# Two fp32 products of a state-space layer become three fp32r passes, and the step is reordered

## The reference

```python
cb = jnp.einsum('bclgn,bcsgn->bclsg', cc, bc)
y_diag = jnp.einsum('bclsgr,bcsgrp->bclgrp', cb[..., None] * decay, xdt)
states = jnp.einsum('bclgn,bclgr,bclgrp->bcgrpn', bc, decay_to_end, xdt)   # "state" product
...
def step(carry, inp):
    st, dec = inp
    return carry * dec[..., None, None] + st, carry
...
y_off = jnp.einsum('bclgn,bcgrpn,bclgr->bclgrp', cc, prev, jnp.exp(a_cs))  # "offset" product
y = (y_diag + y_off) + d_skip * xs; y = y * silu(z); y = rms_norm(y)
```

## Time and profile before

| | |
|---|---|
| median of 3 runs | 2752.06 us (2752.05 to 2752.53) |
| profiled execution, its own time | 2754.46 us |
| its span | 2752.7 us |
| TensorE busy | 2710.4 us, 98% of the span |
| VectorE, ScalarE, GpSimd busy | 58%, 45%, 40% |
| mean granted TensorE clock | 0.997 of full |

### The profile page before, as it was taken

The page is one execution under the profiler, slowest core; times in us unless marked ns, Lnnn a source line. Parts: engine busy times, 40 slices in busy tenths (PEclk is TensorE's granted clock), DMA queues, the critical chain, the costliest instruction groups (busy, mean ns, idle before and its releaser), DMA issues.

```text
span 2752.7 us, 37252 instructions
## 1 busy us (share of the span) xinstructions
PE 2710.4 (98%) x13950; PEld 2234.5 (81%) x13950; DVE 1609.6 (58%) x2221; ACT 1234.6 (45%) x2414; POOL 1093.3 (40%) x798
## 2 busy tenths in 40 slices
PE   8999999999999999999999999999999999999998
PEld 6778778888788887888888888878888888888887
DVE  3589833567425665147763466664445666666666
ACT  2367734556424555145552644555445322222323
POOL 1356641132101322003324587865655435353434
PEclk9999999999999999999999999999999999999999
DMA  9687576645556445565436546674444942333323
GB/s 291 206 272 235 198 273 246 240 161 197 182 200 260 157 148 204 198 233 208 167 144 244 189 157 224 238 265 166 154 141 167 350 153 92 138 122 131 122 92 153
DMA packets 225490, 531.12 MB, mean 193 GB/s; under 512 B 14090, under 2 KB 98062, under 8 KB 215838
## 3 DMA queue, kind: packets, MB, share of 16 engines
q1 hardware_dynamic: 225310, 528.74, 53.6%
HBM read 382.74 MB, written 145.95 MB: 192 GB/s over the span
## 4 chain that ended last, share of the span: by engine, by line
PE 92%; ACT 2%; DVE 2%; DMA 1%; issue 1%; POOL 1%; SPq 0%; DVEq 0%; ACTq 0%; POOLq 0%
PE bank L2007 22%; PE bank L1975 21%; PE bank L1697 19%; PE bank L1741 13%; PE bank L1721 6%; PE bank L1819 2%; PE bank L1812 2%; PE bank L1638 1%; PE bank L1793 1%; PE bank L1800 1%; PE bank L1776 1%; ACT E L1388 1%; DMA w_scr<-w_both 1%; PE bank L1760 1%; PE bank L1930 0%
## 5 line engine op out<-in xcount | busy, mean ns | idle before, releaser
L1697 PE MATMUL bank<-hnT_hi,w_ring 128*128 128x512 f32 x1152 | 374.4, 396 | 1.4 <-DMA w_ring<-w_scr 1.3
L2126 DVE SCALAR_TENSOR_TENSOR acc<-pre,par,acc 128x512 f32<-128x512 f32 x240 | 216.3, 901 | 108.7 <-ACT pre L1250 103.0
L2007 PE MATMUL bank<-w_first,T_hi 128*128 128x512 f32 x896 | 276.0, 389 | 0.3 <-issue 0.3
L1697 PEld LDWEIGHTS bank<-hnT_hi,w_ring 128*128 128x128 f32 x1152 | 216.5, 188 | 46.5 <-ACT pre L1250 1.4
L1975 PE MATMUL bank<-T_hi,w_both 128*128 128x512 f32 x768 | 242.6, 390 | 0.6 <-DMA T_lo<-hn_scr 0.4
L1741 PE MATMUL bank<-w_ring,T_hi 128*128 128x512 f32 x768 | 242.0, 396 | 0.0
L2449 DVE TENSOR_TENSOR acc_th<-bank,acc_th 128x512 f32<-128x512 f32 x224 | 149.9, 686 | 153.5 <-PE bank L2007 153.3
L1003 POOL TENSOR_TENSOR small<-small 128x1 f32<-128x1 f32 (+1 forms) x71 | 17.4, 245 | 546.2 <-ACT yo L1333 340.0
L1697 PE MATMUL bank<-hnT_lo,w_ring 128*128 128x512 f32 x576 | 224.8, 390 | 0.0
L1721 PE MATMUL bank<-w_ring,hnT_hi 128*128 128x384 f32 x768 | 198.4, 339 | 0.0
L2007 PEld LDWEIGHTS bank<-w_first,T_hi 128*128 128x128 f32 x896 | 168.1, 188 | 35.6 <-issue 0.7
(11 more groups left out here) (289 smaller groups left out, 6242.5 us busy)
## 6 DMA issues: line engine op xcount, KB each, us to landing
w_ring<-w_scr SPq DMA_DIRECT2D x312, 512.0 KB, 4.2
T_scr<-stage SPq DMA_DIRECT2D x32, 1792.0 KB, 6.8
w_scr<-w_both SPq DMA_DIRECT2D x104, 512.0 KB, 4.3
pair_raw<-in_w_ff SPq DMA_DIRECT2D x36, 1024.0 KB, 5.5
third<-T_scr SPq DMA_DIRECT2D x28, 1024.0 KB, 4.9
pair_raw<-T_scr SPq DMA_DIRECT2D x28, 1024.0 KB, 4.8
sums<-sums_scr SPq DMA_DIRECT2D x64, 384.0 KB, 4.9
raw<-in_w_in SPq DMA_DIRECT2D x36, 512.0 KB, 6.9
```

The lines of the kernel that those rows point to most:

```text
L1697: mm = nc.tensor.matmul(bank[s][:, :], w[:, k, :], t[:, k, :], start=(k == 0 and j == 0), stop=(k == KT - 1 and j == 2))
L2007: mm = nc.tensor.matmul(bank[4 * half + t][:, :], a[:, k, tok], w[:, k, :], start=(SECOND[q % 7] not in GOES_ON and k == 0 and j == 0), st ...
L2126: ins = nc.vector.scalar_tensor_tensor(acc[:, s, 0:TB], pre[:, s, k:k + TB], w, acc[:, s, 0:TB], ALU.mult, ALU.add)
```

## The change

The state and the offset product each become three fp32r matmuls: high by high, high by low, low by high. The high parts are copies by ScalarE into fp32r tiles (B from the transposed bank, C, S and xw); the low parts are subtractions, B and xw on VectorE, C and S on GpSimd. `y_offset` of q waits for `s_split_lo`, the low part of S of step q; the state product waits for `xw_split_lo`. On TensorE the transposes of y move to one step later and to before the diagonal product, and the state product moves behind `slot1`, so that the fp32 work of a step stands in one piece. GpSimd's decay of S moves up to right behind the split. `state_add` moves ahead of the taps. The copies of the pool history go from VectorE to ScalarE. The split tiles lie in the space of h, so h is loaded during the output projection, behind the weights of its fifth unit.

```diff
 ScalarE, step q
-                        state_ps.wait(act, b, q)
                         ty_ready.wait(act, b, q)
                         xw_ready.wait(act, b, q)
-                        nc.scalar.activation(xb[:, :], bank[4 + q % 2][:, :], ACT.Copy
+                        nc.scalar.activation(b_both[q % 2][:, 0, :], bank[4 + q % 2][:, GW:GW + P],
+                                             ACT.Copy)
+                        nc.scalar.activation(xb[:, :], bank[4 + q % 2][:, 0:GW], ACT.Copy
                                              ).then_inc(xb_ready.sem, 1)
...
                         if q:
                             y_squares(b, q - 1)
+                        yoff_ps.wait(act, b, q)
+                        nc.scalar.activation(c_both[:, 0, :], group_tile(g, 1)[:, c * P:(c + 1) * P],
+                                             ACT.Copy)
+                        state_ready.wait(act, b, q)
+                        nc.scalar.activation(s_both[:, 0, :], S[:, g, :], ACT.Copy
+                                             ).then_inc(s_split_hi.sem, 1)
                         tanh(b, n1)
                         if q:
                             y_norm(b, q - 1)
+                        xw_ready.wait(act, b, q + 1)
+                        nc.scalar.activation(xw_both[:, 0, :], xw[:, :], ACT.Copy
+                                             ).then_inc(xw_split_hi.sem, 1)
...
-                        if q:
-                            y_high(b, q - 1)
+                        if q > 1:
+                            y_high(b, q - 2)
 GpSimd, step q (the inverse root of q-1 stands ahead of it, unchanged)
-                        steps.link(nc.gpsimd.tensor_tensor(by_head(ty[:, :]), by_head(xb[:, 0:GW]),
+                        steps.link(nc.gpsimd.tensor_tensor(by_head(ty[:, :]), by_head(xb[:, :]),
                                                            per_head(dsk, 0, g), ALU.mult))
+                        s_split_hi.wait(pool, b, q + 1)
+                        nc.gpsimd.tensor_tensor(c_both[:, 1, :], group_tile(g, 1)[:, c * P:(c + 1) * P],
+                                                c_both[:, 0, :].bitcast(F32), ALU.subtract)
+                        nc.gpsimd.tensor_tensor(s_both[:, 1, :], S[:, g, :],
+                                                s_both[:, 0, :].bitcast(F32), ALU.subtract
+                                                ).then_inc(s_split_lo.sem, 1)
+                        gains_ready.wait(pool, b, 1)
+                        s_split_lo.wait(pool, b, q + 1)
+                        nc.gpsimd.tensor_tensor(by_head(S[:, g, :]), by_head(S[:, g, :]),
+                                                per_head(cd, c, g), ALU.mult
+                                                ).then_inc(scd_ready.sem, 1)
 TensorE
-                def y_offset(b, q, g, c):
-                    state_ready.wait(pe, b, q)
-                    nc.tensor.matmul(bank[7][:, 0:GW], group_tile(g, 1)[:, c * P:(c + 1) * P],
-                                     S[:, g, :], start=True, stop=True).then_inc(yoff_ps.sem, 1)
+                def y_offset(b, q):
+                    s_split_lo.wait(pe, b, q + 1)
+                    for j, (i, o) in enumerate(((0, 0), (0, 1), (1, 0))):
+                        mm = nc.tensor.matmul(bank[7][:, 0:GW], c_both[:, i, :], s_both[:, o, :],
+                                              start=(j == 0), stop=(j == 2))
+                    mm.then_inc(yoff_ps.sem, 1)
...
+                def state(b, q):
+
+                    xw_split_lo.wait(pe, b, q + 1)
                     yo_ready.wait(pe, b, q + 1)
-                    nc.tensor.matmul(bank[7][:, 0:GW], xb[:, GW:GW + P], xw[:, :],
-                                     start=True, stop=True).then_inc(state_ps.sem, 1)
+                    for j, (i, o) in enumerate(((0, 0), (0, 1), (1, 0))):
+                        mm = nc.tensor.matmul(bank[7][:, 0:GW], b_both[q % 2][:, i, :],
+                                              xw_both[:, o, :], start=(j == 0), stop=(j == 2))
+                    mm.then_inc(state_ps.sem, 1)
...
                         if n1 is not None:
                             unit(b, n1)
+                        if q > 1:
+                            y_transposes(b, q - 2)
                         if q:
-                            slot3(b, q - 1)
+                            diagonal(b, q - 1)
                         slot1(b, q, g, c)
+                        if q:
+                            state(b, q - 1)
                         for n in n2:
                             unit(b, n)
-                        y_offset(b, q, g, c)
-                        if q:
-                            y_transposes(b, q - 1)
-                    slot3(b, STEPS - 1)
+                        y_offset(b, q)
+                    y_transposes(b, STEPS - 2)
+                    diagonal(b, STEPS - 1)
+                    state(b, STEPS - 1)
 VectorE
                             y_finish(b, q - 1)
+                            state_add(b, q - 1)
                         taps(b, n1)
-                        if q:
-                            state_add(b, q - 1)
...
+                        nc.vector.tensor_tensor(b_both[q % 2][:, 1, :], bank[4 + q % 2][:, GW:GW + P],
+                                                b_both[q % 2][:, 0, :].bitcast(F32), ALU.subtract)
...
+                        if n1 is not None:
+                            xw_low(b, q)
                         yoff_ps.wait(dve, b, q + 1)
 SyncE, output projection
+                            if (d, i) == (0, 4):
+                                yoff_ps.wait(sp, b, STEPS)
+                                state_ps.wait(sp, b, STEPS)
+                                sp.dma_start(h[:, :, :], x_in[0, b * TB:(b + 1) * TB, :].rearrange(
+                                    "(t p) d -> p t d", p=P)).then_inc(h_loaded.sem, 16)
```

More of the change, by code:

```diff
@@ L97, in __init__, with mark, wait, link @@
         self.eng, self.sem, self.n = eng, sem, 0
-    def link(self, ins):
+    def mark(self, ins):
         self.n += 1
         ins.then_inc(self.sem, 1)
-        self.eng.wait_ge(self.sem, self.n)
+        return self.n
+    def wait(self, n):
+        self.eng.wait_ge(self.sem, n)
+    def link(self, ins):
+        self.wait(self.mark(ins))
 ITEMS_G = 5 + CH
@@ L201, in build @@
         E = nc.alloc_sbuf_tensor_at("E", [P, HEADS_PER_GROUP, P], F32, offset=T_lo_at)
-        xb = sb("xb", [P, GW + P])
+        xb = sb("xb", [P, GW])
         xdt = sb("xdt", [P, GW])
@@ L245, in build @@
         quad = at("quad", [P, 4, 4, TB], R0 + 32768)
+        s_both = at("s_both", [P, 2, GW], h_at, F32R)
+        xw_both = at("xw_both", [P, 2, GW], h_at + 3072, F32R)
+        c_both = at("c_both", [P, 2, P], h_at + 6144, F32R)
+        b_both = [at(f"b_both{i}", [P, 2, P], h_at + 7168 + 1024 * i, F32R) for i in range(2)]
         t1_at = at("t1_at", [P, 4, TB], R0 + 65536)
@@ L350, in build @@
         g_ready = sig("g_ready", STEPS)
+        s_split_hi = sig("s_split_hi", STEPS)
+        s_split_lo = sig("s_split_lo", STEPS)
+        xw_split_hi = sig("xw_split_hi", STEPS)
+        xw_split_lo = sig("xw_split_lo", STEPS)
         yoff_ps = sig("yoff_ps", STEPS)
@@ L390, in build @@
         f_sumsq, f_rstd, f_out, out_stored = sem("f_sumsq"), sem("f_rstd"), sem("f_out"), sem("out_stored")
-        dve_sem, pool_sem = sem("dve_step"), sem("pool_step")
+        dve_sem, pool_sem, act_sem = sem("dve_step"), sem("pool_step"), sem("act_step")
         rows_loaded, consts = sem("rows_loaded"), sem("consts")
@@ L1048, in _ @@
                                                 ).then_inc(ty_ready.sem, 1)
[L1050 to L1055, removed]
                     inverse_root(b, rsy[:, :], ssy[:, :], ssy_ready, STEPS, rsy_ready, 1)
@@ L1220, in _ @@
                 high_part(act, 1)
+                steps = Steps(act, act_sem)
                 def evac(b, v):
@@ L1243, in evac @@
                         w3 = par[:, W_CONV + 60 + ct:W_CONV + 61 + ct]
-                        nc.scalar.activation(pre[:, s, 0:3], hist[:, ct, :], ACT.Copy
-                                             ).then_inc(hist_read.sem, 1)
+                        hist_read = steps.mark(nc.scalar.activation(
+                            pre[:, s, 0:3], hist[:, ct, :], ACT.Copy))
                         nc.scalar.activation(acc[:, s, 0:TB], ps, ACT.Identity, scale=w3,
                                              bias=par[:, W_BIAS + ct:W_BIAS + ct + 1])
-                        hist_read.wait(act, b, sum(conv_tile(m) is not None for m in range(n + 1)))
+                        steps.wait(hist_read)
                         nc.scalar.activation(hist[:, ct, :], ps[:, TB - 3:TB], ACT.Copy)
@@ L1256, in evac @@
                     else:
-                        nc.scalar.activation(pre[:, s, 16:16 + TB], ps, ACT.Copy
+                        i = n - U_POOL
+                        hist_read = steps.mark(nc.scalar.activation(
```

(32 more changed lines are left out.)

5 lines of the change are left out of this document (removed).

## The result

The changed kernel takes 2912.23 us (2909.14 to 2912.62, 4 runs) against 2752.3: slower, ratio 1.0576, interval 1.0563 to 1.0589. The forecast was 2859, its range 2800 to 2925. The span of its profiled execution is 2910.8 us, 158.1 more than before.

A forecast was written before the change was run, and what follows sets the result against it. The prediction took TensorE as the bound, busy 2710 of 2753 us. From 2754.5 it took 29 saved, added 121 of waiting and 15 of clock, giving 2861.5; the median runs 2.4 lower, so 2859, range 2800 to 2925.

The forecast's parts named there:

- What TensorE saves, 29 us: TensorE, mixer: shorter products and joined fp32 work save 0.40 a step, 26 us; no transpose wait, 3 us; in all 29.
- the one piece of fp32 work: TensorE, each mixer step: fp32 work in one piece instead of two saves 0.05 us, bounded by 0 and 0.15.
- The transposes no longer wait, 3 us off: TensorE, blocks 1 to 3: transposes of y, one step later, lose their 0.35 us wait in nine steps, 3 us off.
- The offset product's wait, 121 us: TensorE, mixer: the offset product waits for S's low part, 2.05 us behind ty's end; 121 us of new waiting together.
- No later step makes it up: Mixer: no later step recovers the new waiting, since each chain starts anew at the end of a step's n1 unit.
- The clock, 15 us: TensorE, blocks 1 to 3: nine stalls of 3.85 us each lose 1.68 us to the lower clock, 15 us.
- a rival of mine (42 us on top): TensorE: the clock also falls at stalls of 2.2 and 2.55 us, 42 us more, 2901 us; chance 0.15.
- Collisions: GpSimd's low parts of C and S: VectorE beside them adds 0 to 1.1 us for the pair, taken as 0.3.
- The rest: VectorE's added work and late h are covered, adding nothing; if not, at most 13 us in block 0 and 22 us.
- h late: Output projection: the later load of h is hidden; if not, 5.5 us in each of four blocks, 22; rival's chance 0.07.

The follow-up runs named there:

- e10: Block 0's mixer as before the change (h still late), blocks 1 to 3 as in e8: 2737.0 us, ratio 0.9944 to the kernel before.
- e11: e10 with both products in fp32 and no splits in blocks 1 to 3 as well, order kept: 2744.02 us, ratio 0.9966 to the kernel before.
- e1: Changed kernel with the new order alone, both products in fp32 and nothing split: 2819.85 us, ratio 1.024 to the kernel before.
- e3: Changed kernel with the high and low part of y moved earlier on ScalarE and VectorE, TensorE's order as changed: 2865.17 us, ratio 1.0405.
- e2: Changed kernel with the transposes of y back behind the offset product, fp32 work in two pieces: 2883.43 us, ratio 1.0468.
- e4: Changed kernel with C and S split, and S decayed, ahead of the inverse root and ty: 2869.69 us, ratio 1.0417.
- e7: Kernel before the change with only h loaded late, behind the fifth unit's weights of the output projection: 2751.96 us, ratio 0.9997.
- e8: e5 with y's high part ahead of the scaling, its low part ahead of xw's, decay of S behind ty: 2773.55 us, ratio 1.0076.
- e5: Changed kernel with the edits of e3 and e4 together: 2808.33 us, ratio 1.0204 to the kernel before.

## Why the prediction was right, and where not

The direction, the first of the two causes and the range held. The sum was 53 us short. That the range held is partly luck: the offset product's wait was put 46 us too high, and the transposes' wait of 62, which the sum had at nothing, came in its place. These steps of the sum were off:

- *What TensorE saves, 29 us.* Three passes do take about 0.52 (0.53 from 578.90 to 579.43 in e10). But the step without a wait, the fourth chunk, is only 0.27 shorter than before (16.86 us against 17.13): 17 us for 64 steps, where I had 0.40 each. With the order held equal (e10 against e11) the passes give 0.27 and not 0.35, and the one piece of fp32 work gives 0.02 (e11 against before) and not 0.05. One item that I left out of the latter: the three transposes, now ahead of the diagonal product, take 0.42 to it (637.95 to 638.37), where they took 0.24 before.
- *The transposes no longer wait, 3 us off.* This step failed. The transposes do not wait for the scaled y, true, but they wait for the bank, which `y_low` of q-3 must have read, and that stands at the end of VectorE's step behind yo and the taps of n2: 62.2 us. Before the change a whole step lay between the two; now only the unit n1 does, and the last groups have none. I named what was queued behind each new wait and not what the moved instruction itself already waited for. e1 shows it by itself (59.0 us without any split), e3 takes it away.
- *The offset product's wait, 121 us.* Measured 74.7. The mechanism was right. Behind the end of ty come 2.06 us in the step shown, where the sum has 2.05, partly by luck: 0.2 of that was for the copy of B, which stands ahead of ty, and the collisions took 0.51 where I took 0.3. Mis-sized was when ty ends: 7.14 us after the diagonal product began, and not 8.24, as in the kernel before. 0.83 of the difference is a collision that changed sides: the inverse root took 0.55 in place of 0.83 and ty 0.83 in place of 1.38, while VectorE's `xdt` beside them took 1.16 in place of 0.55. The rest is mainly that the transposes now stand ahead of the diagonal product. Per step in blocks 1 to 3, groups 1 to 3: 1.4, 1.7, 2.5 and 0 for the four chunks where I had 1.2, 2.55, 3.85 and 0. In the last groups, 1.5 reckoned, it was 0.3, since TensorE had already waited some 2 us at the transposes; where that wait is all but gone it was 0.8 (e3) and 1.0 (e2). Block 0 had 1.35 in place of 2.2.
- *No later step makes it up.* None did, but the offset product's wait and that of the transposes are not independent: in e2, e3 and e4 a third to two thirds of a wait that was removed came back in the other one. How much of that is the loop and how much the edits' own doing is open.
- *The clock, 15 us.* TensorE's busy time rose by 36.8 us although the work shrank by some 17: about 54 us lost to the lower clock. The mean granted clock says the same, 61 us against 8. I counted only stalls like the one of 3.32. The clock fell also behind many idle times of 2.0 to 2.8. It was a rival of mine (42 us on top) that came closest. The rule of the Trainium skill ("TensorE: Matmul & The Clock Gate", section "Why this matters for your kernels"), which asks for no long idle gaps between matmul bursts, agrees with the trace; here shorter ones cost as well.
- *Collisions.* C's and S's low parts take 0.66 and 1.31 beside VectorE, 0.46 and 1.00 without, 0.51 for the pair where I took 0.3. The rule of the Trainium skill ("SBUF — State Buffer", section "SBUF: two separate sides") on the shared port pair agrees with that.
- *The rest.* h late is hidden (e7). Block 0 is fuller than I held: with the orders that free blocks 1 to 3 it is still 31 us longer than before (e8), and 33.7 us of waits stand there at the same two products; the work of VectorE alone I had put at 13 us at most. That VectorE (87% busy there before) and GpSimd have no room is how this and the last section's lines read; shown is that undoing the change in block 0 alone removes the loss (e10).

Of the 158.1 us: 74.7 offset product, 62.2 transposes, 54 clock, less 17 of passes, less 10 of waits that before had (the offset product for S, the state product for yo, the transposes for y); the sum is 164. Some 5 of the other 6 are further idle times of TensorE, which are a little shorter than before. The 54 and the 17 add up to the growth of the busy time by construction, so this sum tests the waits alone.

## What to carry to other kernels

Before an instruction is moved up in an engine's list, read each wait it already carries, buffers that must be free among them, and count what covered it. Where two waits follow each other in every step, mend both and look again: here the gain of either alone was less than its length. And a change that adds work to the helpers can pay in the stages with room (blocks 1 to 3 here, 0.6% faster with e10, order and passes together) and cost in the one without, so decide it stage by stage.

## What the runs showed of the hardware that was not expected

The granted clock fell to its lower level for some 3.4 us, which is 1.7 us of work lost, behind many idle times of TensorE shorter than the 3.32 of before: 2.09 and 2.39 us in blocks 1 to 3, and in the last groups 1.99 with another 0.54 shortly ahead of it. But not behind each: in the changed kernel 2.37 us in block 3 left it at full, as did 1.49 us in the step shown.

```profile
756.41 0.80 PE L1828 MATMUL bank<-s_both,c_both 128*128 128x384 f32 x3 [0.54 <-POOL s_both L1060]
759.19 0.52 PE L1836 MATMUL bank<-ident,y 128*128 128x128 f32 x3 [1.99 <-DVE T_lo L2273]
...
1451.00 0.79 PE L1828 MATMUL bank<-s_both,c_both 128*128 128x384 f32 x3 [2.37 <-POOL s_both L1060]
```

The granted clock was 0.53 from 759.70 to 763.30 and 1.00 from 1451.00 to 1458.00.

VectorE's three taps took 5.94 us in place of 2.32 where GpSimd's weight part and ty stood beside them, in block 0 of e5:

```profile
209.66 2.38 POOL L513 TENSOR_TENSOR w_both<-raw,w_both 128x1024 fp32r<-128x1024 f32 x1 [2.84 <-ACT w_both L505]
...
210.87 5.94 DVE L2173 SCALAR_TENSOR_TENSOR acc<-pre,par,acc 128x512 f32<-128x512 f32 x3 [0.93 <-ACT pre L1269]
...
212.00 1.46 POOL L1071 TENSOR_TENSOR ty<-ty,yo 128x384 f32<-128x384 f32 x1
...
213.43 2.83 POOL L513 TENSOR_TENSOR w_both<-raw,w_both 128x1024 fp32r<-128x1024 f32 x1
...
218.25 2.32 DVE L2173 SCALAR_TENSOR_TENSOR acc<-pre,par,acc 128x512 f32<-128x512 f32 x3
```

GpSimd's work there is back to back for 6.6 us, and the taps end 0.55 us behind it. A late weight part on one engine so delayed everything behind the taps on the other.
